# One inference step on one core: x loaded in blocks of 128, 128 and 32 rows, one activation table for the first norm, 96 small products on an idle TensorE, and channel 0's taps and copy ahead of the constants

## The reference, cut to what matters

```
h    = rmsnorm(x) * norm1_g                       # first norm
proj = h @ w_in                                   # q,k,v,xb,y,ga,gb: seven blocks of 2048 columns
xc   = conv_b + sum_tap xb[t - 3 + tap] * conv_w[tap]      # causal convolution, 4 taps
r, i = sigmoid(xc_blk @ wa + ba), sigmoid(xc_blk @ wx + bx)   # 16 channel blocks of 128
a    = exp(8 * r * log_sigmoid(lambda))           # recurrence h_t = a*h_(t-1) + u
x   += (sigmoid(ga) * (attention @ w_pa) + sigmoid(gb) * ((gelu(y) * h_seq) @ w_pb)) @ w_o
x   += mixture of 16 experts (rmsnorm(x))         # top group, top 2 of 4 experts
y    = rmsnorm(x) * final_norm_g
```

## Time and profile before

| | |
|---|---|
| median of 3 runs | 1700.39 us (1697.88 to 1701.4) |
| the profiled execution's own time | 1699.97 us |
| its span in the profile | 1698.1 us |
| PE busy | 1615.9 us, 95% of the span |
| PEld, DVE, ACT, POOL busy | 1298.9, 721.6, 640.6, 135.6 us |
| HBM | 388.53 MB read, 13.43 MB written, 237 GB/s over the span |

### The profile page before, as it was taken

One profiled execution on the slowest core, in us unless ns is written; L12 is line 12 of the kernel. 1 busy time (PEld: TensorE's weight loads), 2 busy tenths in 40 slices (PEclk: granted clock), 3 DMA queues, 4 the chain that ended last, 5 costly groups with the idle time before them and its releaser, 6 DMA issues. The chain is left out here.

```text
span 1698.1 us, 27524 instructions
## 1 busy us (share of the span) xinstructions
PE 1615.9 (95%) x10710; PEld 1298.9 (76%) x10710; DVE 721.6 (42%) x1073; ACT 640.6 (38%) x1077; POOL 135.6 (8%) x186
## 2 busy tenths in 40 slices
PE   5999999999999999999999999999899999989885
PEld 4999999999999999999999999999634334324221
DVE  5888886443445445545444444543310211111101
ACT  6666665333344444444443333543201211111202
POOL 1544441000000000000000000000000000000000
PEclk9999999999999999999999999999899999999998
DMA  8466556566756546645577666558899999999996
GB/s 213 117 167 162 153 161 176 148 177 169 189 146 184 161 137 172 174 134 160 115 197 191 178 167 176 154 169 336 300 352 398 421 398 420 417 404 421 422 421 243
DMA packets 403751, 399.03 MB, mean 235 GB/s; under 512 B 19456, under 2 KB 377200, under 8 KB 377760
## 3 DMA queue, kind: packets, MB, share of 16 engines
q1 hardware_dynamic: 390912, 383.05, 68.7%
q0 software_dynamic: 2336, 10.23, 2.1%
q10 hardware_dynamic: 10432, 4.79, 1.1%
HBM read 388.53 MB, written 13.43 MB: 237 GB/s over the span
## 5 line engine op out<-in xcount | busy, mean ns | idle before, releaser
L1132 PE MATMUL bank<-hH,wH 128*128 128x288 f32 x1792 | 537.5, 300 | 6.2 <-ACTq L778 2.8
L1564 DVE TENSOR_TENSOR wL<-ring,wH 128x1024 fp32r<-128x1024 f32 x320 | 388.1, 1230 | 356.3 <-ACT wH L715 348.7
L715 ACT ACTIVATE wH<-ring 128x1024 fp32r<-128x1024 f32 x320 | 336.1, 1059 | 521.2 <-PE bank L1134 455.1
L1133 PE MATMUL bank<-hL,wH 128*128 128x288 f32 x1792 | 529.7, 296 | 0.0
L1134 PE MATMUL bank<-hH,wL 128*128 128x288 f32 x1792 | 529.3, 295 | 0.0
L1132 PEld LDWEIGHTS bank<-hH,wH 128*128 128x128 f32 x1792 | 338.3, 189 | 13.4 <-issue 6.9
L1133 PEld LDWEIGHTS bank<-hL,wH 128*128 128x128 f32 x1792 | 338.4, 189 | 0.4
L1134 PEld LDWEIGHTS bank<-hH,wL 128*128 128x128 f32 x1792 | 337.9, 189 | 0.0
L1364 PE MATMUL bank<-raw,hgs 128*64 128x512 f32 x1024 | 242.8, 600 | 18.5 <-DMA raw<-in_expert_w_up 14.9
L1364 PEld LDWEIGHTS bank<-raw,hgs 128*64 128x64 f32 x1024 | 66.5, 136 | 162.9 <-issue 112.5
L1132 PE MATMUL bank<-oH,wH 128*128 128x288 f32 x512 | 150.7, 294 | 0.5 <-DVE oL L1661 0.5
(11 more groups left out here) (303 smaller groups left out, 1539.4 us busy)
## 6 DMA issues: line engine op xcount, KB each, us to landing
raw<-in_expert_w_up SPq DMA_DIRECT2D x128, 1024.0 KB, 26.7
ring<-in_w_in SPq DMA_DIRECT2D x112, 1024.0 KB, 6.6
raw<-in_expert_w_down SPq DMA_DIRECT2D x64, 1024.0 KB, 26.7
ring<-in_w_pb SPq DMA_DIRECT2D x16, 1024.0 KB, 8.9
ring<-in_w_pa SPq DMA_DIRECT2D x16, 1024.0 KB, 9.2
ring<-in_w_o SPq DMA_DIRECT2D x16, 1024.0 KB, 6.0
cK<-in_cache_k SPq DMA_DIRECT2D x16, 256.0 KB, 2.8
cV<-in_cache_v SPq DMA_DIRECT2D x16, 256.0 KB, 3.2
```

The costliest lines, as they stand in the source:

```text
L715: a.activation(wH[2 * (slot % 2) + half][:, :, :], ring[slot][:, 8 * half:8 * half + 8, :], ACT.Copy).then_inc(hi_ready, 1)
L1132: pe.matmul(dst, hi, rH[:, k, :], start=(k == 0), stop=False)
L1133: pe.matmul(dst, hi, rL[:, k, :], start=False, stop=False)
L1564: v.tensor_tensor(lo[:, :, :], ring[slot][:, 8 * half:8 * half + 8, :], hi[:, :, :].bitcast(F32), ALU.subtract).then_inc(lo_ready, 1)
```

## The change

It makes four edits.

- **x in natural blocks.** `x0` and `xn0` have 128 partitions; SP loads rows 0 to 127, rows 128 to 255 and the 32 sample rows, in three DMAs. Squares, roots, scaling and `turn` go by `ROWS = [128, 128, 32]`, with `ssq0`, `rms0`, `rstd0` of their own.
- **One table.** ACT runs one `Sqrt` on `eps_t` in front of its wait for x, and then per block a square and a root.
- **96 small products.** TensorE runs 80 products of `ident16` with `mask16` (128x128, bf16, into `acc[0]`) between its wait for `consts2` and its wait for the parameters, and 16 more behind the parameters' transposes.
- **Channel 0 ahead of the constants.** ACT copies tile 0's product into `xpad` behind the split of tile 1 and in front of `Abs` and `Exp`; DVE copies channel 0's taps and history in front of the 17 instructions of the constants. For channels 1 to 15 the order is as it was.

```diff
             for f in range(2):
-                sp.dma_start(x0[:, f, :], xp[:, f, :]).then_inc(x_in[f], 16)
-            sp.dma_start(x0[0:TAIL, 2, :], xp_tail).then_inc(x_in[2], 16)
-            sp.dma_start(x0[TAIL:TB, 2, :], x_sample[0]).then_inc(x_in[2], 16)
+                sp.dma_start(x0[:, f, :], x_prompt[0, f * P:(f + 1) * P, :]).then_inc(x_in[f], 16)
+            sp.dma_start(x0[0:TS, 2, :], x_sample[0]).then_inc(x_in[2], 16)
...
+            def root(f):
+                r = ROWS[f]
+                a.activation(xn0[0:r, f, :], x0[0:r, f, :], ACT.Square, accum_out=ssq0[0:r, f:f + 1]).then_inc(ssq_ready, 1)
+                a.wait_ge(ssq_ready, f + 1)
+                a.activation(rms0[0:r, f:f + 1], ssq0[0:r, f:f + 1], ACT.Sqrt,
+                             bias=eps_t[0:r, :], scale=1.0 / D).then_inc(rms_ready, 1)
             a.wait_ge(consts, NCONST)
+            a.activation(warm[:, 0:1], eps_t[0:TB, :], ACT.Sqrt)
             for f in range(FT):
-                a.wait_ge(x_in[f], 16 if f < 2 else 32)
-                square_sums(f, xn0, x0)
-                roots(1, (f,))
+                a.wait_ge(x_in[f], 16)
+                root(f)
...
             split(1, 1, 1)
+            def taken(n, tile):
+                a.wait_ge(half_done, 2 * (tile + 1))
+                need(a, xc_ready, n)
+                need(a, tails_ready, 2 * n)
+                a.activation(xpad[:, HIST:HIST + TP], acc[0][:, 0:TP], ACT.Copy).then_inc(xb_ready, 1)
+                a.activation(xpad[:, XW - TS:XW], acc[0][:, TP:T], ACT.Copy).then_inc(xb_ready, 1)
+                a.wait_ge(xb_ready, 2 * n + 2)
+                a.sem_inc(acc_used[0], 1)
+            taken(0, T_LRU)
             own.link(a.activation(lz[:, 0, :], prm2[:, C_LAM:C_LAM + KT], ACT.Abs))
...
             pe.wait_ge(consts2, NCONST2)
+            for _ in range(80):
+                pe.matmul(acc[0][:, 0:P], ident16[:, :], mask16[:, :], start=True, stop=True, skip_group_check=True)
             pe.wait_ge(par_in, 16 * 9)
             pe.transpose(tr[0][:, 0:P], prow[:, :], ident[:, :])
             pe.transpose(tr[1][:, 0:NP2], prow2[:, :], ident[0:NP2, 0:NP2]).then_inc(par_ps, 1)
+            for _ in range(16):
+                pe.matmul(acc[0][:, 0:P], ident16[:, :], mask16[:, :], start=True, stop=True, skip_group_check=True)
...
             split(1, 1)
+            def taps(n, b):
+                need(v, xc_ready, n)
+                v.tensor_copy(cw[:, b, :], taps3[:, :, ds(n, 1)]).then_inc(cw_ready, 1)
+                v.tensor_copy(xpad[:, HIST + TP:HIST + TP + HIST], hist3[:, :, ds(n, 1)]).then_inc(cw_ready, 1)
+            taps(0, 0)
             v.wait_ge(par_ready, 2)
             own.step(v.tensor_scalar(hb[:, :], prm[:, C_BA:C_N1], 0.5, None, ALU.mult))
```

More of the change, by code:

```diff
@@ L178, in build @@
     first4 = sb("first4", [TB, 4])
-    eps_t = sb("eps_t", [TB, 1])
+    eps_t = sb("eps_t", [P, 1])
     warm = sb("warm", [TB, 4])
@@ L183, in build @@
     gup = sb("gup", [P, KT])
+    ssq0 = sb("ssq0", [P, FT])
+    rms0 = sb("rms0", [P, FT])
+    rstd0 = sb("rstd0", [P, FT])
     ssq = sb("ssq", [TB, FT])
@@ L256, in build @@
     here[0] = at_o
-    x0 = sb("x0", [TB, FT, D])
-    xn0 = sb("xn0", [TB, FT, D])
+    x0 = sb("x0", [P, FT, D])
+    xn0 = sb("xn0", [P, FT, D])
     assert here[0] <= at_mixed
@@ L759, in lru @@
                     ahead(T_LRU, 4, i, 2 * b)
[L760 to L766, removed]
                     prev = not (isinstance(n, int) and n == 0)
                     if prev:
+                        taken(n, tile)
                         if isinstance(n, int) and n == 1:
@@ L925, in row_squares @@
                 return src
-            a.activation(warm[:, 0:1], eps_t[:, :], ACT.Sqrt)
+            a.activation(warm[:, 0:1], eps_t[0:TB, :], ACT.Sqrt)
             for m in range(KT):
@@ L938, in _ @@
             a.wait_ge(ssq_ready, FT + 1)
-            a.activation(rms[:, :], ssq[:, :], ACT.Sqrt, bias=eps_t[:, :], scale=1.0 / D).then_inc(rms_ready, 1)
+            a.activation(rms[:, :], ssq[:, :], ACT.Sqrt, bias=eps_t[0:TB, :], scale=1.0 / D).then_inc(rms_ready, 1)
             a.wait_ge(x1_ready, KT - 1)
             a.activation(x1[:, :, (KT - 1) * P:], tail, ACT.Copy).then_inc(x1_ready, 1)
-            a.activation(warm[:, 1:2], eps_t[:, :], ACT.Exp)
+            a.activation(warm[:, 1:2], eps_t[0:TB, :], ACT.Exp)
             a.wait_ge(group_ready, 1)
@@ L950, in _ @@
             a.activation(r1[:, 1, :, :], r1[:, 0, :, :], ACT.Exp).then_inc(ed_ready, 1)
-            a.activation(warm[:, 2:3], eps_t[:, :], ACT.Silu)
+            a.activation(warm[:, 2:3], eps_t[0:TB, :], ACT.Silu)
             def drain_spread(q):
@@ L975, in finish_root @@
                 a.wait_ge(ssqy_ready, nth + 1)
-                a.activation(rmsy[:, column, 1:2], rmsy[:, column, 0:1], ACT.Sqrt, bias=eps_t[:, :], scale=1.0 / D)\
+                a.activation(rmsy[:, column, 1:2], rmsy[:, column, 0:1], ACT.Sqrt, bias=eps_t[0:CAP, :], scale=1.0 / D)\
                  .then_inc(rmsy_ready, 1)
@@ L1042, in _ @@
             y_hi(NE - 1)
-            a.activation(warm[:, 3:4], eps_t[:, :], ACT.Sqrt)
+            a.activation(warm[:, 3:4], eps_t[0:TB, :], ACT.Sqrt)
             a.wait_ge(y_out, 32 * (NG - 1))
@@ L1099, in _ @@
             pe.transpose(tr[1][:, 0:NP2], prow2[:, :], ident[0:NP2, 0:NP2]).then_inc(par_ps, 1)
+            for _ in range(16):
+                pe.matmul(acc[0][:, 0:P], ident16[:, :], mask16[:, :], start=True, stop=True, skip_group_check=True)
             def turn(dst, src, k):
-                for f in range(FT):
-                    ins = pe.transpose(dst[:, f * TB:(f + 1) * TB], src[:, f, k * P:(k + 1) * P], ident[0:TB, 0:TB])
+                for f, r in enumerate(ROWS):
+                    ins = pe.transpose(dst[:, f * P:f * P + r], src[0:r, f, k * P:(k + 1) * P], ident[0:r, 0:r])
                 return ins
@@ L1569, in ahead @@
                 split(base + size * i + u + 2, (u + 2) % RING, halves)
[L1571 to L1583, removed]
+            for f in range(FT):
+                r = ROWS[f]
+                v.wait_ge(rms_ready, f + 1)
+                own.link(v.reciprocal(rstd0[0:r, f:f + 1], rms0[0:r, f:f + 1]))
+                v.tensor_scalar(xn0[0:r, f, :], x0[0:r, f, :], rstd0[0:r, f:f + 1], None, ALU.mult).then_inc(xn_ready, 1)
             split(0, 0)
@@ L1613, in lru @@
                     n = 2 * i + b
-                    need(v, xc_ready, n)
-                    v.tensor_copy(cw[:, b, :], taps3[:, :, ds(n, 1)]).then_inc(cw_ready, 1)
-                    v.tensor_copy(xpad[:, HIST + TP:HIST + TP + HIST], hist3[:, :, ds(n, 1)]).then_inc(cw_ready, 1)
+                    if not (isinstance(n, int) and n == 0):
+                        taps(n, b)
                     ahead(T_LRU, 4, i, 2 * b)
```

## The result

The changed kernel takes 1705.24 us (median of 8 runs, 1704.4 to 1706.55), the kernel before in the same measurement 1700.79 (8 runs, 1697.88 to 1703.45): ratio 1.0028, 95% interval [1.0018, 1.0039]. It is slower by 4.5 us, and lies above the predicted range. The profiled execution took 1706.55 us, the longest of the eight, with a span of 1704.7, 6.6 more than before. Its mean granted clock is 0.982, against 0.992 before, but the two don't compare: the clock's record has no entry before its first change and counts as 1.00 until then, up to 28.1 us before and up to 8.6 after.

A forecast was written before the change was run, and what follows sets the result against it. PE, busy 95% of the span, was taken to bound the kernel. Wait 1.8 and clock fall 1.73 removed, wait 3.4 and fall 1.73 added, the rest 0: net +1.6 us, median 1702.0, range 1696.2 to 1704.4.

The forecast's parts named there:

- x in blocks of 128, first half: the landing: Loading of x at the start: same bytes and queue, rows 0 to 127 in at 12.8 us; cost 0.
- the ring: Load of tile 0, on which ACT's split waits until 18.70 us: landing unchanged, 0, between -0.6 and +0.6.
- Second half: the k steps: Tile 0 on PE: first product at 22.6 us, k steps of about 1.25 us there, cost 0.
- One table: 0: ACT's table loads before x lands: both lie ahead of the landing at 12.8 us, so they give 0.
- 96 products: 0: PE before tile 0: small products of 0.10 to 0.12 us each, hidden, not holding the clock up; 0.
- Rival C: Small products keep PE's clock up to the first dense product: -2.6, net -1.0 us, 1699.4; chance 0.12.
- Channel 0 ahead: +1.6: Tiles 1 to 3: 1.8 us wait for POOL's convolution goes, 3.4 us wait ahead of tile 2 comes; net +1.6.
- the clock's fall: PE's clock drops behind the old wait and behind the new one alike, costing 1.73 us each time.
- Rival B: DVE's constants are not hindered by POOL's convolution: -3.1 us, 1697.3; chance 0.20.
- One to one to the end: What PE gains or loses in the first 60 us reaches the kernel's end in full.
- The sum: Whole kernel: removed 1.8 and 1.73, added 3.4 and 1.73, the rest 0; net +1.6 us, median 1702.0.
- the parts named for slower: Chances of ending over 1703.8 us, from slow small products, a longer clock fall and the forecast's tail: 0.16.

The follow-up runs named there:

- the halves: The changed kernel with each x block of 128 rows loaded by two DMAs of 64 partitions: 1708.99 us (one run).
- Padding: The changed kernel with the third transpose of each k on all 128 partitions and 128 columns, zeros below row 32: 1695.23 us, ratio 0.9977.
- filling: The changed kernel, 32-partition transposes kept, with 45 small products for 16 and 30 more behind the first nine transposes: 1695.28 us, ratio 0.9966.
- two kernels with and without them: The changed kernel with the third transpose on 128 partitions and constants behind tile 2's split, with 96 small products 1691.38 us, without 1691.52.
- 155 products: The changed kernel with third transpose on 128 partitions, constants behind tile 2's split, and 80, 45 and 30 small products: 1689.31 us, ratio 0.9929.
- the two padded kernels: The changed kernel with the third transpose on 128 partitions, once with the 96 small products (1695.23 us), once without (1694.75 us).

## Why the prediction was wrong

**x in blocks of 128, first half: the landing.** The prediction said: "The bytes are the same and so is the queue", so block 1 at 12.8 and the ring still at 18.70. Shown wrong: block 1 at 8.86, the ring's split at 14.73. The rate of one DMA depends on its partitions, and the halves undo it. The landing of 11.0 us was taken as the queue's pace; that it was the pace of 96 partitions none of its rows showed. The trace of before had the sign, in the experts, whose weights come by DMAs of 1 MB to 128 partitions in rows of 8 KB (the last column is GB/s):

```profile
1300.00:1400.00 100.00, 97.12 (x447) 35.53 (x444) 15.80 (x34) 18.00 (x34) 2.87 (x3) 1.00 1.02 412
```

The faster landing was worth -3.96 us at the first product, beyond the lower bound of -0.6.

**Second half: the k steps, and here the forecast fell.** The prediction kept "k steps of about 1.25 us there" and cost 0. The transposes were counted only by their number, three for each k. They went from three of 96 partitions to two of 128 and one of 32; the steps took 1.69 and stayed so. This is the term that was put at nothing: tile 0 took 9.6 us more, and with 3.96 won ahead of it tile 1 started 5.64 late. Padding (-8.7 us by the ratios) and filling (-10.5) each take it away or most of it, and without the products it stays; so the cause is the 32-partition transpose, by its own cost (3.1 us against padded steps) and by a clock that doesn't rise under it (8.4). Why a load of 32 partitions stands back was only read: the Trainium skill (TensorEngine Tiling (Array Packing), section "Key Properties") says that a change of tiling mode drains the engine, and it lists tiles of 32 rows among the modes. That a transpose of 32 partitions between others of 128 is such a change is an inference. The 0.33 and 0.17 us ahead of each such load, and none ahead of the 96-partition ones, agree with it. No run here separates the drain from another reason for the 32 partitions. Nor is shown why the clock doesn't rise; five kernels with that transpose and no full cover ahead of it had 1.69 twelve times, and in all five the clock came up behind the last of these transposes. Of those with 96 or 128 partitions none had more than five slow steps.

**One table: 0.** Nothing shows against it; ACT waited 0.75 us for block 1 and 1.04 for the ring behind it. It had no experiment of its own.

**96 products: 0.** Right as far as the runs can tell, and for the reason given: the clock fell at about 15.4, ahead of the first product, in the changed kernel, and two kernels with and without them agree (1691.38, 1691.52); alone they gave 1.0007. They took 0.076 us each, below the 0.10 to 0.12 taken, and ended at 11.6. What the prediction left open, whether transposes can hold the level, is answered for padded ones: with nothing else ahead of it the clock rose at 18.1 behind twelve of them in one kernel, and in another only at 22.7. Rival C, the clock held up to tile 0, was a question of how much idle time is filled: with 155 products it came true, worth 2.1 us by the steps, near its 2.6.

**Channel 0 ahead: +1.6.** Right in the main: the `xc` wait gone, the wait at tile 2 3.04 for 3.4 (2.85 in the kernel with the move alone), two small instructions per POOL instruction, a fall behind it. Alone it measured +1.7 (0.2 to 3.2). What was too sure is the clock's fall. Behind the old gap it came in the profile of before (1.8 us), not in three others with 1.82, 1.31 and 1.03. Behind the new one it came in four of seven profiles, and it cost 1.3 to 1.5 us each time, not 1.73. Where the old fall doesn't come and the new one does, the move costs 2.0 to 2.9 by the ratios, so part of the agreement of 1.6 with 1.7 is luck. Rival B is refuted by the row of 2.79 us.

**One to one to the end.** It held to the experts within 1.1 us (7.05 late at tile 7, 8.1 ahead of them): their first products behind the wait for `xs` start 9.34 us late, 1.3 of it in that wait itself. In the experts 2.7 came back, where PE waited 22.2 us for weights instead of 25.6.

**The sum.** The medians of the single parts, by their ratios, are +0.7 (x), +1.7 (move) and +1.2 (products), together 3.6; the change has 4.8. With intervals of about 1.5 us to each side these agree. Open stays why x alone costs so little when its timeline is 3.8 us late at tile 7. In its profile the lateness goes in the experts, where PE waited 3.6 us less for weights; that this holds for the other executions is not shown. A small slip stands in the chances too: the parts named for slower add up to 0.15, not 0.16.

## What to carry to other kernels

When a block is cut anew, ask of every instruction that reads it how many partitions it now has, in the DMA, which ran at about half the rate with 96 or 64 instead of 128, and in TensorE's transposes, where one of 32 between others of 128 cost 9.6 us where the load had won 4.0. Here the odd rest was cheaper padded to the full shape. And the chain of small DVE instructions, put beside POOL's work, took twice as long (2.79 us for seven instead of 1.44): put behind what TensorE waits for next, it cost nothing, and both the old wait and the new one were gone.

## What the runs showed of the hardware

- One DMA to 128 partitions of 8 KB rows ran at 418 to 430 GB/s, to 96 at 234 to 238, to 64 at 213 to 217, with the engines' share at 1.0 in all three. A packet of 8 KB took 309, 552 to 562 and 594 to 596 ns.
- Three transposes with weights of 96 partitions took 0.39 us at the lower level; two of 128 and one of 32 took 0.80; at the higher level three of 128 took 0.25 and the mixed three 0.48.
- At 0.50, 23 us of dense work, 20 of them with the mixed transposes in it, didn't bring the clock up; at 1.00 the same work kept it. Twelve padded transposes without any product had the clock up at 18.1 us in one kernel, not in another.
- A gap doesn't decide the clock by its length alone: behind 3.04, 3.10 and twice 2.85 us it fell, behind 2.86 and 2.84 in the two padded kernels and 2.50 in the one with x by halves it stayed at 1.00, and behind 1.8 it did both.
- The clock column has no entry before its first change: before reads 1.00 from 22 to 28 us, where products took 0.61 and 0.59 us, the lower level's durations (0.40 and 0.38 at the higher). There only the durations tell.
